# Page loads of the key/value compression on two queues, three slots each, and its stores on the SyncE queue

## The reference, cut to what matters

```python
def gather_pages(pool, page_table):
    g = pool[page_table]
    return g.reshape((g.shape[0], g.shape[1] * g.shape[2]) + g.shape[3:])

def nsa_compress(rows, pe, w1, w2):            # rows (B, L, 2 heads, 64)
    r = CMP_LEN // CMP_STRIDE                  # 32 // 16
    n_chunk = L // CMP_STRIDE
    n_cmp = n_chunk - r + 1
    ch = rows[:, :n_chunk * CMP_STRIDE].reshape(B, n_chunk, CMP_STRIDE, G, D)
    blk = jnp.concatenate([ch[:, j:j + n_cmp] for j in range(r)], axis=2)
    blk = blk + pe[:, None, :].astype(blk.dtype)
    flat = jnp.swapaxes(blk, 2, 3).reshape(B, n_cmp, G, CMP_LEN * D)
    return jax.nn.silu(flat @ w1) @ w2         # 2048 -> 128 -> 64
```

## Time and profile before

| what | value |
|---|---|
| median of 3 runs | 5908.55 us (5907.72 to 5920.07) |
| profiled execution, its own time | 5905.93 us |
| its span in the trace | 5904.3 us |
| PE busy, share of the span | 74% |
| DVE, ACT, POOL busy | 29%, 19%, 4% |
| stage "cmp", first load issued to the last store issued | about 734 to 1440 us |

### The profile page before, as it was taken

One profiled execution on the slowest core, in us unless ns is written; L12 is line 12 of the kernel. 1 busy time (PEld: TensorE's weight loads), 2 busy tenths in 40 slices (PEclk: granted clock), 3 DMA queues, 4 the chain that ended last, 5 costly groups with the idle time before them and its releaser, 6 DMA issues. The chain is left out here.

```text
span 5904.3 us, 71278 instructions
## 1 busy us (share of the span) xinstructions
PE 4381.6 (74%) x20295; PEld 2900.8 (49%) x20295; DVE 1735.8 (29%) x5006; ACT 1104.9 (19%) x2271; POOL 227.5 (4%) x348
## 2 busy tenths in 40 slices
PE   5799989998988556666654455659956868788869
PEld 4344477876555345434433344335544544444434
DVE  1100133332455320222222111521124643433422
ACT  1100022222566100111110000120002532212211
POOL 0000000000000000000000000300001110000000
PEclk9999989998799555777765555779956988898989
DMA  1535143332223112233210111421132215455442
GB/s 46 200 144 188 56 119 109 112 110 74 70 69 86 37 30 62 86 93 100 89 55 24 33 39 50 167 70 66 54 93 74 66 58 175 147 173 168 142 151 100
DMA packets 401933, 558.94 MB, mean 95 GB/s; under 512 B 71010, under 2 KB 283814, under 8 KB 399921
## 3 DMA queue, kind: packets, MB, share of 16 engines
q1 hardware_dynamic: 368572, 489.93, 26.5%
q0 software_dynamic: 11712, 36.27, 2.1%
q10 hardware_dynamic: 21408, 29.85, 1.4%
HBM read 494.13 MB, written 118.25 MB: 104 GB/s over the span
## 5 line engine op out<-in xcount | busy, mean ns | idle before, releaser
L266 PE MATMUL PS<-even_w,even_xT 128*128 128x512 f32 (+3 forms) x1296 | 533.4, 573 | 15.2 <-DMA even_w<-in_w_in_e 9.3
L925 PE MATMUL PS<-cmp_xT,cmp_w 128*128 128x255 f32 (+2 forms) x2176 | 491.2, 377 | 1.1 <-DVEq L1004 1.1
L925 PEld LDWEIGHTS PS<-cmp_xT,cmp_w 128*128 128x128 f32 x2176 | 397.6, 194 | 47.7 <-issue 1.2
L266 PEld LDWEIGHTS PS<-even_w,even_xT 128*128 128x128 f32 (+1 forms) x1296 | 233.9, 182 | 314.2 <-issue 306.7
L829 ACT ACTIVATE cmp_xT<-PS 64x512 f32<-64x512 f32 x260 | 155.3, 597 | 1045.8 <-PE PS L896 1044.3
L266 PE MATMUL PS<-odd_w,odd_xT 128*128 128x368 f32 (+1 forms) x1008 | 315.5, 475 | 11.9 <-DMA odd_w<-in_w_in_o 7.7
L829 DVE COPY cmp_xT<-PS 64x512 f32<-64x512 f32 x260 | 179.3, 690 | 352.0 <-PE PS L896 350.0
L1655 PE MATMUL PS<-s_fox_kT,s_fox_qz 128*128 128x512 f32 x512 | 267.7, 649 | 0.0
L1699 PE MATMUL PS<-s_fox_kv,s_fox_S 128*64 128x256 f32 x1024 | 246.8, 397 | 14.9 <-issue 14.5
L266 PEld LDWEIGHTS PS<-odd_w,odd_xT 128*128 128x128 f32 (+1 forms) x1008 | 182.2, 182 | 144.7 <-issue 40.1
L1646 PE MATMUL PS<-ident,s_sel_kv 128*128 128x128 f32 x512 | 119.7, 379 | 159.9 <-DMA s_sel_kv<-in_cache_nsa 157.1
(11 more groups left out here) (442 smaller groups left out, 6254.6 us busy)
## 6 DMA issues: line engine op xcount, KB each, us to landing
s_fox_kv<-in_cache_fox SPq DMA_DIRECT2D x512, 256.0 KB, 4.1
cmp_pairs<-in_cache_nsa SPq DMA_DIRECT2D x512, 128.0 KB, 2.8
s_sel_kv<-in_cache_nsa SPq DMA_DIRECT2D x512, 128.0 KB, 2.2
out_dil_sample<-in_cache_dil_w SPq DMA_DIRECT2D x8, 4088.0 KB, 22.0
even_w<-in_w_in_e SPq DMA_DIRECT2D x8, 2048.0 KB, 8.0
HE<-even_o ACTq DMA_DIRECT2D x64, 256.0 KB, 2.1
odd_w<-in_w_in_o SPq DMA_DIRECT2D x7, 1472.0 KB, 6.4
HO<-odd_o ACTq DMA_DIRECT2D x56, 184.0 KB, 1.9
```

The costliest lines, as they stand in the source:

```text
L266: last = nc.tensor.matmul(PS[0:size(t), bank * 512:bank * 512 + n], xT[:, k, t * 128:t * 128 + size(t)], w[:, half, k, 0:n], start=(k == 0 ...
L925: last = nc.tensor.matmul(hidden_ps(x, NK)[:, g], w1[:, kv, c, :], xT[:, u % 2, kv, g, c % 8, at:at + NK], start=(c == 0), stop=(c == 15))
```

## The change

The loading of a slot and the storing of a unit become functions `load(eng, n)` and `store(eng, u)`. SP loads the slots of even number, POOL those of odd number, so that each has three of the six places. Both wait for `turned` as before. The stores move from POOL to SP: the stores of unit u stand behind the load of the fourth slot (q = 3) of unit u + 3, and those of the last three units behind all loads. SP instead of POOL waits in the end for all stores. PE, DVE and ACT execute the same instructions in the same order.

```diff
+        def load(eng, n):
+
+            u, q = source[n]
+            b, h = units[u][0], units[u][1]
+            x = n % SLOTS
+            if n >= SLOTS:
+                eng.wait_ge(turned, 2 * (n - SLOTS) + 2)
+            if b is None:
+                for i in range(4):
+                    eng.dma_start(pairs[:, x, i], E.HE[256 * i:256 * i + 256, KCMP:KCMP + 256].rearrange("(p l) w -> p l w", l=2)).then_inc(p_in[x], 16)
+            else:
+                at = 32 * h + 8 * q
+                _, pages = nc.values_load_multi_w_load_instructions(E.page_table[b:b + 1, at:at + 8], engines=(eng.engine,),
+                                                                    min_val=0, max_val=N_POOL - 1)
+                for i in range(8):
+                    eng.dma_start(pairs[64 * (i % 2):64 * (i % 2) + 64, x, i // 2],
+                                  pages_of[ds(pages[i], 1), :, 0:256].rearrange("x (p l) w -> (x p) l w", l=2)).then_inc(p_in[x], 16)
+
+        def store(eng, u):
+            b, h, _, NK = units[u]
+            for kv in range(2):
+                eng.wait_ge(made, 2 * u + kv + 1)
+                dst = (E.kc_p, E.vc_p)[kv] if b is None else (E.kc_s, E.vc_s)[kv][b]
+                at = 255 * h
+                for i in range(2):
+                    n = min(128, NK - 128 * i)
+                    if n > 0:
+                        eng.dma_start(dst[at + 128 * i:at + 128 * i + n], res[0:n, u % 2, kv, i]).then_inc(stored[u % 2], 16)
...
-                for n, (u, q) in enumerate(source):
...
+                for n in range(0, len(source), 2):
+                    load(sp, n)
+                    for u in range(NU):
+                        if n in (first_group[min(u + 3, NU)] + 3, first_group[min(u + 3, NU)] + 4):
+                            store(sp, u)
+                for u in range(NU - 3, NU):
+                    store(sp, u)
+                sp.wait_ge(zero_out, 32)
+                for x in range(2):
+                    sp.wait_ge(stored[x], sum(32 if units[u][0] is None else 64 for u in range(NU) if u % 2 == x))
...
-                for u, (b, h, _, NK) in enumerate(units):
-                    for kv in range(2):
-                        pool.wait_ge(made, 2 * u + kv + 1)
...
+                for n in range(1, len(source), 2):
+                    load(pool, n)
```

## The result

The changed kernel took 5842.89 us (median of 4 runs, 5822.83 to 5862.39) against 5908.14 us for the kernel before (median of 4). The ratio is 0.9886, with a 95% interval of 0.985 to 0.9922: 1.1% faster. The forecast was 5838 us with a range of 5829 to 5861. The profiled execution ran 5822.83 us, the fastest of the four, so a comparison of the two traces shows more (83 us) than the medians do (65 us).

What follows compares the result with a forecast made beforehand. SP's sequencer, issuing page loads at 10.15 us a slot, was taken to bound the kernel. Gains 63.0 + 2.6 + 6.3 - 1.0 = 70.9 us; 5905.93 - 70.9 = 5835.0, median 2.6 above: 5838 us, range 5829 to 5861.

Steps and rivals of the forecast that it cites:

- SP's pace and PE's own: Compression, slot 5 to slot 64: SP needs 10.15 us a slot, PE 9.1; two queues gain 63.0 us.
- The recorded idle time: Case within a rival: only PE's recorded 50.2 us of page waits, 740 to 1420 us, go; 5858 us.
- POOL's slot: Page loads on POOL: taken at 11 us a slot, between 9.3 and 20.3, hidden up to 18.0 us.
- The clock: Slot 4 to about 799 us: without PE's wait the granted clock doesn't fall; 6.3 us gained, at the least nothing.
- Slot 4: Early in the compression: slot 4 becomes SP's second page slot, so PE's wait for it goes; 2.6 us gained.
- Contention at the start: Stage start: POOL's first slot loads beside SP's weights, for which PE waits; 1 us lost, between 0 and 1.7.
- The end of the stage: Stage end: two stores of 1.08 us on SP instead of POOL, then the same wait for landing; costs nothing.
- The sum: Whole kernel: 63.0 + 2.6 + 6.3 - 1.0 = 70.9 us gained, forecast 5838 us; chance 0.46.
- the clock falls all the same: Rival, stage start: the clock still falls, perhaps from unit 0's small products; 64.6 us gained, 5844 us; chance 0.28.
- transfers bind: Rival, page loads: a second queue gains nothing, 5908 us; chance 0.05, shared with POOL just at 20 us.
- POOL starves: Rival, POOL's loads: DVE's work holds up its DMA instructions, 25.5 us a slot, 6078 us; chance 0.07.
- another wait is next: Rival, PE's turns: copies of ACT and DVE or a slower POOL limit the gain, 5858 or 5870 us; chance 0.14.

Runs made afterwards that it cites:

- the experiment that was made for it: The changed kernel with SP loading slot 4 only after the first turn of slot 2; 5846.9 us in one run.

## Why the prediction was right

**SP's pace and PE's own.** I took 10.15 us a slot for SP, 9.1 for PE, and 63.0 us of gain from slot 5 to slot 64, with 0.8 us of clock in it. Measured: 1396.60 - 797.73 = 598.87 us before, 1326.85 - 789.62 = 537.23 after, 61.6 us. PE's unit takes 2 x 18.19 = 36.4 us, against 36.3 reckoned from start to start. The recorded idle time, 50.2 us with slot 4's 2.64 in it, would have been some 13 too low against 61.6 + 2.8 less the clock's 0.8: the ends of matmuls are modelled, and a wait hides behind them in part (0.71 us by starts for a recorded 0.49 in the earlier trace rows).

**POOL's slot.** Taken at 11 us, between 9.3 and 20.3; measured 8.85. It was hidden, as forecast, with 9 us in hand. The upper end came from an issue of 1.41 us and from POOL reading page numbers at twice SP's price; an issue took 0.59 us, and it read them at about SP's price (4.1 against 4.5 us).

**The clock.** Slot 4 came 2.80 us earlier (2.6 forecast). From there to slot 5 it took 5.70 us and not 11.01: 5.3 us for the clock in that piece against 5.5. The other 0.8 us of the term's 6.3 is counted twice in the prediction: the slow turn at 797.73 lies behind the start from which the 63.0 us are measured, and these already take every turn at full clock. Without it the sum would have been 70.1.

That the fall had been caused by the wait is now supported by more than one case, though not by the experiment that was made for it. In the traces of four kernels PE waited longer than 2 us near there, and its turn behind the wait took 1.94 us instead of 1.04: 2.64 us in the kernel before, 4.81 with the stores on SP alone, 7.91 with the page numbers once a unit, and 10.69 with POOL slowed. These are the second and the third:

```profile
797.16 1.94 PE L908 MATMUL PS<-ident,cmp_pairs 128*128 128x128 f32 x8 [4.81 <-DMA cmp_pairs<-in_cache_nsa]
```

```profile
801.96 1.94 PE L912 MATMUL PS<-ident,cmp_pairs 128*128 128x128 f32 x8 [7.91 <-DMA cmp_pairs<-in_cache_nsa]
```

A wait of 1.03 us at 786.47 in the kernel with the stores on SP left its turn at 1.06. In the traces whose PE didn't wait there, the clock stayed up once it had risen.

The middle of the stage has more cases. Over the whole stage these four traces have 22 waits for pages of 2.6 us or more. Behind 20 of them the turn or the group of products that follows ran in part or whole at 1.2 GHz; behind two, of 3.28 and 2.97 us, the clock stayed at 2.4 GHz. None of the 52 waits from 1.0 to 2.03 us at full clock had a fall behind it. So waits of nearly the same length did and did not bring the clock down. Here are a fall and one of the two exceptions, from the kernels with the page numbers once a unit and with the stores on SP:

```profile
915.70 1.94 PE L912 MATMUL PS<-ident,cmp_pairs 128*128 128x128 f32 x8 [2.60 <-DMA cmp_pairs<-in_cache_nsa]
```

```profile
964.74 1.06 PE L908 MATMUL PS<-ident,cmp_pairs 128*128 128x128 f32 x8 [3.28 <-DMA cmp_pairs<-in_cache_nsa]
```

In the middle a fall was short: from the turn behind the wait to the next one it took 5.7 to 6.05 us and not 4.33, so it cost 1.4 to 1.7 us and not 5.3. The Trainium skill (TensorE: Matmul & The Clock Gate, Why this matters for your kernels) advises against idle gaps between bursts of matmuls, because the clock drops behind them. These traces agree, with 20 falls behind 22 such waits.

**Contention at the start.** I took 1 us from 0 to 1.7. From POOL's first instruction of the stage to PE's first transpose of slot 0 it is 13.6 to 13.8 us in the four traces without page loads of POOL at the start (before, stores on SP alone, page numbers once a unit, POOL slowed: 735.3 to 749.1 in the last), and 14.0 to 16.5 us in the seven with such loads and slot 0 behind w1 (733.7 to 747.7 in the changed kernel, 735.0 to 751.5 the longest). So it costs 0.2 to 2.9 us. Only the longest lies above my upper end of 1.7, and that is the one kernel with the extra DVE copies; the other six stand at 14.0 to 15.3.

**The end of the stage** was costed at nothing, and this is the step of the prediction that failed: "two stores of 1.08 us on SP instead of POOL, then the same wait for landing". It gave 6.2 us in the trace (46.1 to 39.9 from last transpose to `pa_qn`). In the two experiments that move loads and stores apart it goes with the queue that stores, and waits for the stores in the end: 47.3 us with POOL, 39.8 with SP.

**The sum.** At the first load of prompt attention the trace is 76.0 us ahead: 69.8 from the stage's terms (70.9 forecast) and 6.2 from its end. By that the median should have come to 5832 us; it came to 5843, and to 5851 when repeated. In the repeated kernel's trace the stage was 75.1 us ahead, and 23.2 us of that were lost in later stages against the trace before, 11.9 of them in the paged attention of layer 1. Stages with unchanged code vary by this much between executions (prompt attention 523 to 536 us over the twelve traces, selected-block attention 732 to 756, paged attention 884 to 900), and of the kernel before there is only one trace. From the first load of prompt attention to the end that trace needed 4458 us, and the eleven others 4451 to 4481, on average 4466. Whether the changed kernel loses some 10 us there by more than chance stays open. So the forecast was right in place and mechanism, but that it came within 5 us of the median is in part luck: 6 us that it left out at the stage's end, and some 10 that went in later stages, nearly cancel.

**The rivals.** That the clock falls all the same is out for the changed kernel: it was full from about 772 us in its trace and stayed so to the stage's end. That transfers bind is out (DMA share 0.43 at PE's full pace). That POOL starves is out. That another wait is next is out: no row of PE's waits for `cmp_xT` copies appeared.

Of the versions tried none is clearly better than the changed kernel: those with PE at its own pace have medians from 5836 to 5851 us, within their spread.

## What to carry to other kernels

Divide the issuing queue's time for one buffer by the consumer's time for it, both read from start to start. While the issuer was the slower one here, every tenth of a microsecond on its sequencer was paid once per buffer, in full (0.5 us more a slot, 30 us later); once it was the faster one, nothing more was to be had, whether that was reached by two queues or by one that needs less for each buffer. And price what a queue does between its DMAs: here reading eight page numbers cost 4.5 us of 10.2, nearly as much as the eight issues (5.6).

## What the runs showed of the hardware that was not expected

- POOL's queue took 8.85 us for a slot of eight page loads with addresses from registers, SP's 10.15. An issue took 0.59 us on POOL (4.74 for eight) and 0.70 on SP (5.6 for eight).
- Reading page numbers into registers grew with their count: 0.88 us for 8, 3.36 us for 32. POOL's sequencer did it while memsets ran on the engine (two of them, 12.3 us together).
- The DMA right behind the 2 MB load of w1 stood 5.3 to 5.4 us on SP's queue, whichever of two DMAs that was (6.3 us with slot 0 going out on ACT's queue beside it).
- With its last stores on POOL's queue the stage needed 9.0 and 10.3 us (two traces) from their issue to the next stage's first load, with SP's queue 3.0 to 3.1 (ten traces).
- The granted clock rose at a different time in each execution at the stage's start, between about 772 and 805 us, behind the same instructions of PE. That alone moved the stage's end by up to 15 us.
- Of 22 waits of PE for pages of 2.6 us or more, 20 were followed by a fall of the granted clock to 1.2 GHz; of 52 waits from 1.0 to 2.03 us at full clock none was.
